# Summing the modulation's accumulators over the array's column quarters, and where the sums and the rounding stand

## The reference

```python
c_act = jax.nn.silu(c)
for l in range(DEPTH):                                   # DEPTH = 2
    ada = c_act @ w_ada[l] + b_ada[l]                    # (1, 6 * 1024)
    sh1, sc1, gt1, sh2, sc2, gt2 = jnp.split(ada, 6, axis=-1)
    h = rms(x, g_mix[l]) * (1.0 + sc1) + sh1
    ...                                                  # projections, attentions, gates
    x = x + gt1 * (mixed @ w_out[l])
    h2 = rms(x, g_mlp[l]) * (1.0 + sc2) + sh2
    x = x + gt2 * (jnp.square(jax.nn.relu(h2 @ w_ff1[l])) @ w_ff2[l])
```

## Time and profile before

| | |
|---|---|
| median of 3 runs | 1552.73 us (1552.14 to 1554.5) |
| profiled execution, its own time | 1550.83 us |
| its span | 1549.0 us |
| PE busy | 1488.4 us, 96% of the span |
| DVE busy | 914.0 us, 59% |
| ACT busy | 627.8 us, 41% |
| POOL busy | 39.0 us, 3% |
| granted TensorE clock, mean | 0.975 |

### The profile page before, as it was taken

The page is one execution under the profiler, slowest core; times in us unless marked ns, Lnnn a source line. Parts: engine busy times, 40 slices in busy tenths (PEclk is TensorE's granted clock), DMA queues, the critical chain, the costliest instruction groups (busy, mean ns, idle before and its releaser), DMA issues.

```text
span 1549.0 us, 20715 instructions
## 1 busy us (share of the span) xinstructions
PE 1488.4 (96%) x8502; PEld 1106.8 (71%) x8502; DVE 914.0 (59%) x1535; ACT 627.8 (41%) x1006; POOL 39.0 (3%) x39
## 2 busy tenths in 40 slices
PE   7999999998999999999699899999999999999998
PEld 6876343335888634433479798898987888889897
DVE  4985111117787511111889878987868976765554
ACT  6443121114334312111555655444455556454443
POOL 0000000000000000000300000000002000000000
PEclk9998999999999999999799999999989999999999
DMA  9877999996473999999665443998934533444540
GB/s 370 310 307 297 421 422 421 421 421 271 163 282 127 423 421 421 420 421 421 234 217 201 153 173 148 355 346 314 367 126 177 190 109 111 162 162 171 184 164 28
DMA packets 58776, 420.23 MB, mean 271 GB/s; under 512 B 6625, under 2 KB 6689, under 8 KB 8370
## 3 DMA queue, kind: packets, MB, share of 16 engines
q1 hardware_dynamic: 58034, 417.19, 68.9%
q0 software_dynamic: 640, 1.61, 0.3%
HBM read 417.73 MB, written 1.05 MB: 270 GB/s over the span
## 4 chain that ended last, share of the span: by engine, by line
PE 84%; DVE 11%; ACT 3%; issue 1%; DMA 0%; SPq 0%; ACTq 0%; DVEq 0%
PE ps L802 81%; DVE lo L1948 2%; DVE AR L1941 2%; ACT AR L1851 1%; PE ps L893 1%; PE ps L1388 1%; DVE ACC L1941 1%; PE ps L1122 1%; PE ps L1359 1%; DVE AR L2575 1%; ACT hi L1510 0%; DVE AR L1938 0%; ACT AR L1759 0%; DMA raw<-in_gla_qk 0%; DVE TINY L2011 0%
## 5 line engine op out<-in xcount | busy, mean ns | idle before, releaser
L1948 DVE TENSOR_TENSOR lo<-raw,hi 128x1024 fp32r<-128x1024 f32 x300 | 367.8, 1248 | 113.7 <-ACT hi L1510 112.8
L1510 ACT ACTIVATE hi<-raw 128x1024 fp32r<-128x1024 f32 x300 | 310.3, 1056 | 202.5 <-PE ps L802 196.4
L802 PE MATMUL ps<-T,hi 128*128 128x256 f32 x1792 | 332.9, 287 | 10.0 <-DVE lo L1948 8.6
L802 PEld LDWEIGHTS ps<-T,hi 128*128 128x128 f32 x1792 | 284.2, 194 | 19.2 <-DVE lo L1948 8.6
L802 PE MATMUL ps<-hi,T 128*128 128x512 f32 x896 | 289.0, 398 | 4.1 <-DVE T L1941 3.0
L802 PE MATMUL ps<-T,lo 128*128 128x256 f32 x896 | 254.8, 284 | 0.0
L802 PEld LDWEIGHTS ps<-hi,T 128*128 128x128 f32 x896 | 171.7, 192 | 40.6 <-issue 5.3
L802 PE MATMUL ps<-lo,T 128*128 128x512 f32 x448 | 176.2, 393 | 0.0
L802 PEld LDWEIGHTS ps<-T,lo 128*128 128x128 f32 x896 | 173.3, 193 | 0.0
L802 PE MATMUL ps<-hi,AF 128*128 128x512 f32 x512 | 166.1, 396 | 0.4 <-DVE AF L2696 0.4
L1941 DVE SCALAR_TENSOR_TENSOR AR<-AR,ps 128x512 f32<-128x512 f32 x52 | 35.3, 684 | 173.0 <-ACT AR L1681 108.1
(11 more groups left out here) (240 smaller groups left out, 1804.4 us busy)
## 6 DMA issues: line engine op xcount, KB each, us to landing
raw<-in_moe SPq DMA_DIRECT2D x76, 1024.0 KB, 14.9
raw<-in_b_ff SPq DMA_DIRECT2D x64, 1024.0 KB, 5.1
AR<-in_moe SPq DMA_DIRECT2D x60, 1024.0 KB, 13.7
raw<-in_ada SPq DMA_DIRECT2D x48, 1024.0 KB, 6.3
ring<-in_moe SPq DMA_DIRECT2D x44, 1024.0 KB, 13.9
raw<-in_b_in SPq DMA_DIRECT2D x24, 1024.0 KB, 6.3
raw<-in_b_gate SPq DMA_DIRECT2D x16, 1024.0 KB, 4.8
ACC<-in_moe SPq DMA_DIRECT2D x12, 1024.0 KB, 16.5
```

The lines of the kernel that those rows point to most:

```text
L802: return e.matmul(o, l, r, start=a, stop=z, skip_group_check=True)
L1510: e.activation(hi[n % NC][:, :], raw[place[c]][:, 1024 * half:1024 * half + 1024], ACT.Copy).then_inc(*to("hi", "hi", n))
L1948: tt(lo[n % NC][:, :], r, hi[n % NC][:, :], SUB).then_inc(*to("lo", "lo", n))
```

## The change

A key's sum is done the other way round. The ones are now the stationary operand, 32 columns wide, and a quarter of the accumulator, 512 columns, moves; quarter j writes partitions 32 j to 32 j + 31 of a bank. ScalarE copies the bank to SBUF (`sum_row`). TensorE transposes it in four pieces (`sum_turn`), and VectorE's `sum_out` picks every 32nd column.

The pieces move. The sums of key (0, 2) and (1, 2) stand behind the attention's last product, those of (1, 0) and (1, 1) behind layer 0's last feed-forward product; the first key's copy stands on ScalarE before the last square, the second's behind it, and the transposes at the head of the norm stage. In the MoE the sum stays behind the router, the copy stands behind the rounding of `x_hi`, the transposes behind gather 3 of the first pair of experts, the addition behind the gates. `ahead(3)` now stands behind the columns. The statistics lose one step: the first addition takes the epsilon with it, and the factor goes into the root's constants.

```diff
 def walk_moe(feed, key):
     ...
     yield ("x_hi", 1)
+    yield ("sum_row", key)
     yield ("ranks",)
     ...
-    yield ("sum_out", key)
     ...
                 yield ("gather", 0, 3)
+                yield ("sum_turn", key)
     ...
                 yield ("gates",)
+                yield ("sum_out", key)
 
 def walk_rms(feed, sums, first):
-    if not first:
-        feed.late = feed.ahead(3)
-        yield from ((x, n) for x, n in feed.late if x == "hi")
-        feed.late = [(x, n) for x, n in feed.late if x == "lo"]
-    yield from (("sum_up", k) for k in sums)
+    yield from (("sum_row", k) for k in sums[1:])
+    yield from (("sum_turn", k) for k in sums)
     yield ("rms",)
     yield from (("sum_out", k) for k in sums)
     ...
     yield from feed.some_late(NC)
+    if not first:
+        yield from feed.ahead(3)
+
+def sums_up(sums):
+    yield from (("sum_up", k) for k in sums)
+    yield from (("sum_row", k) for k in sums[:1])
 
 # between the two sinks of the attention's last product, and in walk_ff:
+            if (t, n) == (1, 1):
+                yield from sums_up(sums)
             yield ("x_out", t, n)
 
 # TensorE
-                for j in range(16):
-                    ins = mm(p[:, j:j + 1], acc[:, 128 * j:128 * j + 128], C["ones"][:, 0:1], True, True)
+                for j in range(4):
+                    ins = mm(p[32 * j:32 * j + 32, :], C["ones"][:, 0:32], acc[:, 512 * j:512 * j + 512], True, True)
+            def sum_turn(key):
+                p = take("sum_turn", key)
+                w.wait_ge(*after("sum_row", key))
+                for j in range(4):
+                    ins = e.transpose(p[:, 128 * j:128 * j + 128], sum_mem(key)[:, 128 * j:128 * j + 128], ident)
+                ins.then_inc(*to("tile", "sum_turn", key))
+                give(("sum_turn", key), "sum_out", key)
 
 # ScalarE
+            def sum_row(key):
+                w.wait_ge(*after("sum_up", key))
+                e.activation(sum_mem(key), PS[bank["sum_up", key]][:, :], ACT.Copy)...
 
 # VectorE
-                tt(ADA[...], PS[bank["sum_up", key]][:, 0:16], VE["b_ada"][...], ADD)
+                tt(columns[0], PS[bank["sum_turn", key]]...[:, :, :, 0], columns[1], ADD)
     ...
-                        tt(ss, SSP[:, :, 0], SSP[:, :, 1], ADD).then_inc(*to("step"))
-                        w.wait_ge(*last("step"))
-                        ts(ss, ss, 1.0 / 1024.0, 1e-6, MUL, ADD).then_inc(*to("step"))
-                        rsqrt(rms, ss, 2, tiny("b_nr", 4)).then_inc(*to("step", "rms", l, blk))
+                        stt(ss, SSP[:, :, 0], 1024.0 * 1e-6, SSP[:, :, 1], ADD, ADD).then_inc(*to("step"))
+                        rsqrt(rms, ss, 2, tiny("b_nr", 4), 32.0).then_inc(*to("step", "rms", l, blk))
```

More of the change, by code:

```diff
@@ L138, in walk_b @@
             for t in range(2):
+                if tail and t:
+                    yield "after", n, ()
                 yield "sink", n, t
@@ L166, in run_a, with run_b @@
             yield from tick()
-def run_b(name, nb, kt, feed, tick=None, half=None, last=None, halved=False, staggered=False):
+def run_b(name, nb, kt, feed, tick=None, half=None, last=None, halved=False, staggered=False, after=None):
     us = []
@@ L184, in run_b @@
             yield from last()
+        elif what == "after" and after:
+            yield from after
         elif what == "sink":
@@ L535, in walk_attention @@
     yield from side.drain()
-    yield from run_b("o", 2, 8, feed, halved=True, staggered=True)
+    yield from run_b("o", 2, 8, feed, halved=True, staggered=True, after=sums_up(sums))
 def spread(which):
@@ L542, in spread, with walk_ff @@
     yield [("spread", which, 1)]
-def walk_ff(feed):
+def walk_ff(feed, sums):
     side = Side(spread(1))
@@ L792, in norm_mem, with sum_mem @@
             return VE["ln_g"][:, 8 * q:8 * q + 8], VE["ln_b"][:, 8 * q:8 * q + 8], (moe_mem.GB if q % 2 else LNG)
+        def sum_mem(key):
+            layer, blk = key
+            return ar(10240 + 512 * (blk % 2), 512) if layer or blk == 2 else moe_mem.GR
         def tensor_program(e):
@@ L1337, in attention @@
                         tile_of[pairs[n] + x] = (n, x // 2)
-                for what, *a in walk_attention(feed):
+                for what, *a in walk_attention(feed, sums):
                     if what == "qkv":
@@ L1422, in attention, with feed_forward @@
                         spread_rows(l, *a)
-            def feed_forward(l):
+                    elif what == "sum_up":
+                        ada_sum(a[0])
+            def feed_forward(l, sums):
                 m = block_mem
@@ L1436, in feed_forward @@
                         take("ff_y", l, t, n)
-                for what, *a in walk_ff(feed):
+                for what, *a in walk_ff(feed, sums):
                     if what == "up":
@@ L1795, in modulate, with attention @@
                         column_hi("rms", (l, blk), a[0])
-            def attention(l):
+            def attention(l, sums):
                 m = block_mem
-                for what, *a in walk_attention(feed):
+                for what, *a in walk_attention(feed, sums):
                     if what == "hi":
@@ L1974, in sum_out @@
                 o = layer * 48 + blk * 16
-                w.wait_ge(*after("sum_up", key))
-                tt(ADA[:, layer, 16 * blk:16 * blk + 16], PS[bank["sum_up", key]][:, 0:16], VE["b_ada"][:, o:o + 16],
+                w.wait_ge(*after("sum_turn", key))
+                columns = [x.rearrange("p (c b) -> p c b", c=4) for x in (ADA[:, layer, 16 * blk:16 * blk + 16], VE["b_ada"][:, o:o + 16])]
+                tt(columns[0], PS[bank["sum_turn", key]][:, :].rearrange("p (b c r) -> p c b r", b=4, c=4)[:, :, :, 0], columns[1],
                    ADD).then_inc(*to("sum", "sum_out", key))
@@ L2790, in gpsimd_program @@
                     pass
-                attention(l)
+                attention(l, [])
                 for _ in walk_rms(feed, [], False):
                     pass
-                for _ in walk_ff(feed):
+                for _ in walk_ff(feed, []):
                     pass
```

48 lines of the change are left out of this document (30 added, 18 removed).

## The result

The changed kernel takes 1538.61 us (median of 4 runs, 1537.15 to 1540.64) beside 1553.62 for the kernel before on the same chip: ratio 0.9902, 95% interval 0.9882 to 0.9922. In two later comparisons it took 1537.41 (0.9893, 0.9852 to 0.9933) and 1538.00 (0.9912, 0.9893 to 0.9931). That is 13 to 17 us less; forecast were 9.5, and 1538.6 lies 0.9 under the stated range. The profiled execution took 1538.3 around a span of 1536.5; those of the two later comparisons have spans of 1534.8 and 1535.5, a second one of the kernel before 1550.1. The ratios are of executions in the faster of the chip's two states, which leaves out one, of moe_quarters_only, at 3764 us.

A forecast was written before the change was run, and what follows sets the result against it. TensorE was taken to bound the kernel, with 84% of the chain of waits. Terms of -4.9, -2.3, -0.75, -0.1, -0.2 and -1.4 gave -9.65, say -9.5: 1543.2 us from 1552.73; own range 1541 to 1546, 8-in-10 range 1539.5 to 1548.

The forecast's parts named there:

- The third stage: Third norm stage: sums leave the path, transposes start at 1150.6 instead of 1155.79; net -4.9 us.
- the statistics' shorter step: VectorE's rms chain in the norm stages loses one dependent step, 0.2 us.
- rounding ahead: Fourth norm stage: rows no longer wait behind ScalarE's rounding, -0.75 us; second stage rounds nothing ahead, nothing to win.
- The head norm's collision with POOL: Layer 1: POOL's table multiplications move 4 us ahead of VectorE's head norm, clearing most of the collision; -2.3 us.
- rival (a): Layer 1's head norm: POOL's drawn-out multiplications still cover it, the collision stays; 1545.5 us, chance 0.18.
- Rival (b): Keys' sums: quarters go in order or pairs, 1546.9 us, chance 0.12; nothing side by side, 1550.8, chance 0.04.
- Rival (c): ScalarE's queue: slow sums delay statistics, 3 us per microsecond of key over 1.05; gain gone from 4.2; chance 0.03.
- The second MoE's zero: Second MoE's routing: an earlier start is lost because TensorE is 0.15 us ahead of starving for last weights; 0.
- Rival (e): First MoE: its gain is lost to its last loads; 1544.6 us, chance 0.05.
- the first MoE's gain: First MoE's routing: the count starts when SEL is there, 129.95 instead of 131.59; -1.4 us, kept through the layer.
- the clock's term: Third norm stage: first projections may still run at half clock; price 0 to 1.5 us, taken as 0.3.
- Rival (d): Norm stages: sums and transposes keep the clock full, first column 0.5 to 0.9 us sooner in three; 1541.0, chance 0.08.

The follow-up runs named there:

- moe_quarters_only: The kernel before with only the two MoEs' keys summed over the column quarters; 1548.98 us, ratio 0.9980.
- one_quarter: The changed kernel with all four products of each blocks' key through the first column quarter, into the same 32 rows; 1547.83 us, ratio 0.9980.
- block_sums_old: The changed kernel with the blocks' four keys summed the old way, ahead of the statistics; 1545.83 us, ratio 0.9952.
- stats_only: The kernel before with the one-operation-shorter statistics alone; 1549.95 us, ratio 0.9998.
- round_ahead: The changed kernel with three half chunks again rounded ahead of the statistics in the second, third and fourth norm stages; 1540.10 us, ratio 0.9932.
- late_tables: The changed kernel with layer 1's head tables on GpSimd waiting for the third norm stage's first four row transposes; 1543.17 us, ratio 0.9952.
- slow_sums4: The changed kernel with each quarter product of the blocks' four keys made four times over; 1548.14 us, ratio 0.9976.
- second_and_heads_busy: The changed kernel with 2 unread products ahead of the second MoE's count and 2 ahead of layer 0's first head transposes; 1537.23 us, ratio 0.9906.
- after: The changed kernel itself, in its first comparison; 1538.61 us, ratio 0.9902.
- after_again: The changed kernel, unchanged, measured again in five more rounds; 1537.41 us, ratio 0.9893.
- before_heads_busy: The kernel before with unread products ahead of the first head transposes, 2 in layer 0 and 3 in layer 1; 1550.01 us, ratio 0.9996.
- moe_sums_old: The changed kernel with the two MoEs' keys alone summed the old way at the old place; 1540.09 us, 2.7 over the changed kernel.
- warm_short: The changed kernel with 3, 2 and 3 unread products ahead of the first row transposes in norm stages two, three and four; 1536.97 us, ratio 0.9909.
- routing_busy: The changed kernel with 2 unread products ahead of each MoE's count and 1 ahead of the first gather; 1537.54 us, ratio 0.9908.
- warm_long: The changed kernel with unread products in long stands: 6 ahead of the layer norm, 14 the first norm stage, 2 each MoE's count; 1552.13 us, ratio 1.0010.

## Why the prediction was off

**Right, by the runs.** The mechanism, and every part's sign. A key takes 1.07 us (1.05 forecast), and one_quarter shows that the overlap makes it; the column quarter and the rows of the bank that it writes are one choice, so that no run tells which of the two the passes would queue for. The third stage gains by the sums' form and place (block_sums_old); the statistics' shorter step is worth nothing that can be measured (stats_only); rounding ahead costs the fourth stage 0.9 (0.75 forecast) and the second nothing (round_ahead). The head norm's collision with POOL is real: -2.1, -2.7 and -2.2 against -2.3, and late_tables brings it back; so rival (a) is out. Rival (b) is out: four passes run at once, neither in pairs nor in line. Rival (c)'s mechanism is there, and its price of 3 us for each microsecond of a key is low: 4.2 by slow_sums4 (10.1 / 2.43) and 3.8 by one_quarter (9.8 / 2.55), head norm and clock included. For the blocks' sums alone the gain of 8.4 is gone near 3 us a key. The second MoE's zero is right for the reason given: an earlier start ends at the last weights' landing (second_and_heads_busy). Rival (e) is out too, since after keeps its 2.3 us ahead at 730. The landing bounds the first MoE's gain too: no profile stands more than 2.3 ahead there.

**Wrong: the clock's term.** The sum has +0.3 us for the clock in the third stage and nothing anywhere else, and takes layer 0's head transposes as untouched; so the forecast was too small, and the range with it. The mean of the three executions differs from the forecast by this: layer 0's head transposes -1.8, first routing -0.9, third stage -0.7, first stage -0.6, second stage -0.5, against +0.7 at the layer norm and the second routing: -3.8, which is the distance from 9.65 to the profiles' 13.4. At two of these places the rows show half clock as what made the difference. At layer 0's head transposes the stand is the same 2.65 us in before and after_again, and all of the 1.6 lies behind it; before_heads_busy, which is the kernel before with that stretch taken away, has -1.5 there. At the first routing after_again starts the count 1.6 us sooner, as forecast; 0.3 more lies between count and gathers, where the count took 1.22 at half clock and takes 0.72, and 0.5 over the gathers, low until 138.3 in before and until 135.2 in after_again.

The size is also not firm. In seven of its nine stretches behind 125 us the table moves between executions of one kernel by 0.6 to 1.3 us, and the sum at the end is between 12.5 and 14.2 in the three. At two places the time went with no edit in the code there: the first routing in moe_sums_old (-1.6, low for 6.9 in place of 10.3 us) and in stats_only (-1.6, the same), of which 1.1 and 1.0 had been lost up to 125 us with the clock full only from 14.6 and 14.4 us instead of 12.0; and layer 0's head transposes in stats_only (-2.1).

Rival (d) had this in part, at 0.08 and at 0.5 to 0.9 us in three stages. Its place was wrong. In the norm stages the columns come last: with or without a low stretch the third is within 0.3 us, the second within 0.7; the fourth loses 1.2 only where a stretch reaches into the dense products. The larger part of the time was at the first routing and at layer 0's head transposes.

**What stays open.** That the whole surplus is the half clock fits its places and the fall from 77 us to 43 to 55. The rows bear it out at the two places above; for the norm stages it is not shown. Taking a stretch away shortened its place in two cases, by 1.5 us at layer 0's head transposes (before_heads_busy) and by 1.9 to 2.7 at the second routing (-2.1 in three kernels beside -0.2 to +0.6 in after). But 1.4 to 3.2 us were lost elsewhere in the same executions, so that no gain could be told in a median (warm_short, before_heads_busy, routing_busy, second_and_heads_busy), and stats_only lost one stretch and got others. Whether the change itself moved the stretches, or only the moment at which each product now comes, is open too. Why layer 0's head transposes have a low stretch in both profiles of before and in warm_long's (797.0 to 800.4, 11 us later like all there), and in none of the others, is not settled either. The Trainium skill, TensorE: Matmul & The Clock Gate, Terms, prices throttled time at that time times the share of clock lost. By that, 77 less 43 to 55 us would be an estimated 11 to 17 us, more than the whole surplus; the stretches lie partly over stands and over work that waits for VectorE, and there warm_short shows a price of nothing.

## What to carry to other kernels

Sums over partitions go through the array as 32-column products with the accumulator moving, one to each column quarter, copied and transposed: 1.07 us for 2048 columns instead of 4 to 5.4, and behind it 0.6 for the copy and 0.45 to 0.64 for the transposes. Put such a sum behind the last dense product and its copy where ScalarE would wait anyway, and look at which other engine waits for the sum. When a forecast adds up shortened stands on TensorE, list each stretch at half clock in the profile, and price it by whether TensorE or another engine ends last behind it: the 3.4 us ahead of a wait for ScalarE cost nothing in before, and the 3.4 us behind it 1.5 in stats_only. Widen the range on the side of the gain by what the bound ones hold. Take a second profile of each kernel before a difference of about 1 us in one stage is put down to an edit.

## What the runs showed of the hardware

- Eight fp32 passes of 128x512 take 1.07 us in four column quarters (four of them at once) and 3.62 in one (0.43 apart).
- Where the clock is low differs between executions of one kernel: 951.6 to 955.1 and 1146.2 to 1149.6 in one execution of after, full in two others. It also rises first at different places: 12.0 us in before, 14.4 in stats_only, 14.6 in moe_sums_old, with 1.0 and 1.1 us lost up to 125 us.
- VectorE's 128x16 steps take 0.66 to 0.79 us beside POOL's multiplications instead of 0.18, and three of them 1.99 instead of 0.47.
- A low stretch of 3.4 us ahead of a wait for ScalarE costs nothing (8.3 us either way); one of the same length behind it costs 1.5 (5.57 against 4.09).
- Full-width fp32 products of 512 columns that nothing reads take 0.91 us each (2.74 for three), and delay nothing in warm_short, where they fit the stand. Two or three of them ahead of the second routing's count and gathers went with a full clock there in all three kernels that had them, where all three executions of the changed kernel have a low stretch between 514 and 525 us. At the first routing they did not help: the clock fell at 133.4 us all the same.
